# Decode attention over cached pages: pages turned in 32x32 blocks on VectorE, block-diagonal queries, one softmax join, and memory keys as fp32 products

## What is computed

```python
# decode tokens: attention over 1024 cached positions (8 pages of 128) and the token itself
q_lat = einsum("bqhe,rhe->bqhr", q_nope, w_uk)              # 256 wide
s_past = einsum("bqhr,bkr->bhqk", q_lat, c_past) + einsum("bqhe,bke->bhqk", q_pe, kpe_past)
s_new  = einsum("bqhr,bkr->bhqk", q_lat, c_new)  + einsum("bqhe,bke->bhqk", q_pe, kpe_new)
p = softmax(concatenate([s_past, s_new], -1) * MLA_SCALE)
o = einsum("bqhr,rhe->bqhe", p_past @ c_past + p_new @ c_new, w_uv)
# prompt: memory keys and values, 256 tokens, 2048 -> 4 heads x 128
mn = rms_norm(mem, norm_mem); mem_k = mn @ w_mk; mem_v = mn @ w_mv
```

## Time and profile before

| | |
|---|---|
| runs of the kernel before | 1203.07, 1203.53, 1209.15 us; median 1203.53 us |
| the profiled execution | 1201.51 us, of which the span from first to last instruction is 1199.8 us |
| granted TensorE clock, mean | 0.992 of full speed |
| DMA | 216.13 MB, mean 180 GB/s |

### The profile page before, as it was taken

How to read it: one execution, slowest core, us unless ns; L and a number is a source line. 1 busy time by engine, 2 the same in 40 slices (tenths; PEclk the granted TensorE clock), 3 DMA queues, 4 the chain that set the end, 5 groups by cost and what they waited for, 6 DMA issues and landing times. The chain is left out here.

```text
span 1199.8 us, 25822 instructions
## 1 busy us (share of the span) xinstructions
PE 1151.4 (96%) x10209; PEld 1062.3 (89%) x10209; DVE 894.3 (75%) x1521; ACT 643.3 (54%) x1130; POOL 172.8 (14%) x282
## 2 busy tenths in 40 slices
PE   7999999999999999998889999999998999999988
PEld 6999999999777899997879999999986779999977
DVE  5689988889767544686587998888997773448745
ACT  7474454545457544565565645444446664446554
POOL 1210101010353000032011010101014510001400
PEclk9999999999999999999989999999999999999999
DMA  7795756464568466687447676655654874667842
GB/s 209 189 264 141 220 136 179 123 186 134 166 189 241 140 183 177 198 252 264 119 114 202 186 190 171 177 150 153 172 150 142 224 212 140 186 184 219 275 176 73
DMA packets 318971, 216.13 MB, mean 180 GB/s; under 512 B 21620, under 2 KB 300512, under 8 KB 318298
## 3 DMA queue, kind: packets, MB, share of 16 engines
q1 hardware_dynamic: 301728, 164.64, 49.9%
q0 software_dynamic: 16800, 49.83, 13.3%
q10 hardware_dynamic: 330, 0.11, 0.0%
HBM read 209.31 MB, written 7.15 MB: 180 GB/s over the span
## 5 line engine op out<-in xcount | busy, mean ns | idle before, releaser
L1341 ACT ACTIVATE whi<-stage 128x2048 fp32r<-128x2048 f32 (+2 forms) x157 | 272.9, 1739 | 276.6 <-PE U L691 234.5
L1963 DVE TENSOR_TENSOR wlo<-stage,whi 128x2048 fp32r<-128x2048 f32 x138 | 315.8, 2289 | 129.8 <-ACT whi L1341 129.6
L689 PE MATMUL U<-Ahi,whi 128*128 128x264 f32 x1152 | 333.3, 289 | 0.7 <-DVE wlo L1963 0.5
L690 PE MATMUL U<-Alo,whi 128*128 128x264 f32 x1152 | 326.9, 284 | 0.0
L691 PE MATMUL U<-Ahi,wlo 128*128 128x264 f32 x1152 | 326.3, 283 | 0.0
L689 PEld LDWEIGHTS U<-Ahi,whi 128*128 128x128 f32 x1152 | 217.4, 189 | 4.5 <-DVE wlo L1963 1.6
L690 PEld LDWEIGHTS U<-Alo,whi 128*128 128x128 f32 x1152 | 217.7, 189 | 0.0
L691 PEld LDWEIGHTS U<-Ahi,wlo 128*128 128x128 f32 x1152 | 216.4, 188 | 0.0
L2140 DVE SCALAR_TENSOR_TENSOR acc<-uext,cwall,acc 128x256 f32<-128x256 f32 x464 | 189.2, 478 | 0.4
L689 PE MATMUL U<-Bhi,whi 128*128 128x264 f32 x384 | 108.9, 284 | 0.0
L690 PE MATMUL U<-Blo,whi 128*128 128x264 f32 x384 | 108.8, 283 | 0.0
(11 more groups left out here) (461 smaller groups left out, 2176.2 us busy)
## 6 DMA issues: line engine op xcount, KB each, us to landing
stage<-in_w_in SPq DMA_DIRECT2D x76, 1024.0 KB, 6.0
stage<-in_w_out SPq DMA_DIRECT2D x32, 1024.0 KB, 5.8
stage<-in_w_mk SPq DMA_DIRECT2D x8, 1024.0 KB, 6.5
cp<-in_cache_kv_latent POOLq DMA_DIRECT2D x64, 128.0 KB, 3.1
cp<-in_cache_kv_latent SPq DMA_DIRECT2D x64, 128.0 KB, 3.0
stage<-in_w_mv SPq DMA_DIRECT2D x8, 1024.0 KB, 5.4
Kt<-in_cache_mem_k POOLq DMA_DIRECT2D x16, 512.0 KB, 6.4
stage<-in_w_xq SPq DMA_DIRECT2D x8, 1024.0 KB, 7.1
```

The lines of the kernel that those rows point to most:

```text
L689: mm(bk[:, 0:cols], whi[:, s, w], hi[:, k, :], start=(k == 0), stop=False)
L690: mm(bk[:, 0:cols], whi[:, s, w], lo[:, k, :], start=False, stop=False)
L1341: return A_(out, in_, ACT.Copy, scale=scale)
L1963: ins = V.tensor_tensor(wlo[:, s, :], stage[:, s, :], whi[:, s, :].bitcast(F32), ALU.subtract)
```

## The change

Decode attention goes by sequence s (a "sample", eight pages) instead of chunks of four sequences. VectorE turns each page in 32x32 blocks (`key_turns`: 2560 elements on each partition a sample, from `rawc` and `rawk` to `KBL` and `KBP`, of which there is one copy). Queries are spread once (`spread_queries`: 40 products with columns of the identity) and copied by ScalarE into `QB`, which POOL has set to zero, so that each block of 32 rows of a 128x32 weight tile holds its queries in its own 8 columns. `scores(s)` then makes 40 products of 64 columns, and every row of the result (page pair, block, head) has its own maximum and sum. Each sample's values go unscaled to `oR[s]`; at the end `stats_turn`, `combine_max`, `combine_weights`, `weights_turn`, `combine_pick` and `latents` join all rows of all samples with the new token's scores. Copies of probabilities and values move from VectorE to ScalarE (`d_probs`, `d_out`). The 8 loads of `dmask` go.

The memory rows stay in fp32 (`memF`, even ones by ScalarE, odd ones by VectorE: `mem_full`), and a quarter of a memory key unit is four fp32 products that take the weights from `stage`. These units are not split; their stage buffers are free when the unit is done. For the memory value units, `memF` is split later, in the loop over output units (ScalarE for m = 4 to 7, VectorE for m = 5 to 8).

The core of the diff:

```diff
-    CPO = ((W, W + 4096), (W + 10240, W + 14336), (M, M + 8704))
-    KRO = (W + 8192, W + 18432, M + 4096)
-    cp = [[at(f"cp{e}_{pp}", [P, 4, KVL], CPO[e][pp]) for pp in range(PP)] for e in range(3)]
-    kr = [at(f"kr{e}", [P, PP, 4, DR], KRO[e]) for e in range(3)]
-    KT = at("KT", [P, 2, 4, KEYS], W + 30336)
-    KTr = at("KTr", [P, 2, KEYS], W + 38528)
-    sD = at("sD", [P, KEYS + NB], W + 40960)
+    RAW = (W, W + 10240, W + 30720)
+    rawc = [at(f"rawc{e}", [P, NPAGE, KVL], RAW[e]) for e in range(3)]
+    rawk = [at(f"rawk{e}", [P, NPAGE, DR], RAW[e] + 8192) for e in range(3)]
+    KBL = at("KBL", [P, NPAGE, RBL, 32], W + 20480)
+    KBP = at("KBP", [P, NPAGE, RBP, 32], W + 28672)
...
         def load(l, u, s, dst, src):
 
-            sp.wait_ge(split_hi.sem, split_hi.at(l, u - NST + 1))
-            sp.wait_ge(split_lo.sem, split_lo.at(l, u - NST + 1))
+            if U_MK <= u - NST < U_MK + 4:
+                sp.wait_ge(unit_done.sem, unit_done.at(l, u - NST + 1))
+            else:
+                sp.wait_ge(split_hi.sem, split_hi.at(l, splits(u - NST)))
+                sp.wait_ge(split_lo.sem, split_lo.at(l, splits(u - NST)))
...
             load_mk(1)
             if l == 0:
-                sp.wait_ge(const_load, 16 * 12)
+                sp.wait_ge(const_load, 16 * 4)
             load_pages(sp, l, 0, 0)
             load_pages(sp, l, 1, 0)
-            load_mk(2)
             load_pages(sp, l, 2, 0)
             load_pages(sp, l, 3, 0)
-            load_mk(3)
+            load_mk(2)
             load_pages(sp, l, 4, 0)
             load_pages(sp, l, 5, 0)
+            load_mk(3)
+            load_pages(sp, l, 6, 0)
             load_out(0)
-            load_pages(sp, l, 6, 0)
+            load_pages(sp, l, 7, 0)
             load_out(1)
-            load_pages(sp, l, 7, 0)
             load_out(2)
...
+            wait_apart(pool, unit_done.sem, unit_done.at(l, U_MK))
+            nc.gpsimd.memset(QB[:, :, :, :], 0.0)
+            nc.gpsimd.memset(pD[:, :, :, :, :], 0.0).then_inc(qb_zero.sem, 1)
...
+            def spread_queries():
+                pe.wait_ge(ql_ev.sem, ql_ev.at(l, 4))
+                pe.wait_ge(qn_ev.sem, qn_ev.at(l, H))
+                pe.wait_ge(ut_ev.sem, ut_ev.at(l, 2))
+                for k in range(RBK):
+                    for i in range(4):
+                        if k < RBL:
+                            sel, q = ident[:, 32 * (k % 4):32 * (k % 4) + 32], QLt[:, k // 4, :, :]
+                        else:
+                            sel, q = ident[0:DR, 32 * (k - RBL):32 * (k - RBL) + 32], QPt[0:DR, :, :]
+                        last = mm(HAB[32 * i:32 * i + 32, 64 * k:64 * k + 64], sel, q, start=True, stop=True)
+                last.then_inc(qb_mm.sem, 1)
...
+            def scores(s):
+                pe.wait_ge(kb_rdy.sem, kb_rdy.at(l, s + 1))
+                if s % 4 == 0:
+                    pe.wait_ge(qb_ev.sem, qb_ev.at(l, s // 4 + 1))
+                if s >= 2:
+                    pe.wait_ge(dex.sem, dex.at(l, s - 1))
+                o = 64 * (s % 2)
+                for k in range(RBK):
+                    for g in range(4):
+                        keys = KBL[:, 2 * g:2 * g + 2, k, :] if k < RBL else KBP[:, 2 * g:2 * g + 2, k - RBL, :]
+                        last = mm(HC[32 * g:32 * g + 32, o:o + 64], QB[:, s, k, :], keys, start=(k == 0), stop=(k == RBK - 1))
...
+            def probs(s):
+                pe.wait_ge(dex.sem, dex.at(l, s + 1))
+                if s >= 2:
+                    pe.wait_ge(dpT_ev.sem, dpT_ev.at(l, s - 1))
+                for t in range(2):
+                    o = 64 * (s % 2) + 32 * t
+                    for i in range(4):
+                        last = mm(HD[32 * i:32 * i + 32, o:o + 32], sD[:, s % 2, 32 * t:32 * t + 32],
+                                  ident[:, :].rearrange("p (g i h) -> p i g h", g=4, i=4)[:, i, :, :], start=True, stop=True)
...
+            def latents():
+                pe.wait_ge(cm_dve.sem, cm_dve.at(l, CM_PICK))
+                pe.wait_ge(do_ev.sem, do_ev.at(l, NB))
                 for c in range(2):
-                    last = tr(HD[:, c * P:(c + 1) * P], oR[:, c * P:(c + 1) * P], ident[:, :])
-                last.then_inc(doT_mm.sem, 1)
+                    w = slice(c * P, (c + 1) * P)
+                    mm(HB[:, c * 64:c * 64 + 64], cnew[:, w], cnd[:, :, :], start=True, stop=False)
+                    for s in range(NB):
+                        last = mm(HB[:, c * 64 + s * H:c * 64 + (s + 1) * H], oR[s][:, w], csel[:, s, :],
+                                  start=False, stop=(s == NB - 1))
+                last.then_inc(cm_pe.sem, 1)
...
+                bk = U[s % 2]
                 if s == 0:
-                    pe.wait_ge(mn_lo.sem, mn_lo.at(l, 14 if k0 == 0 else 16))
-                part(U_MK + s, s, Ahi[:, :, 0:NM], Alo[:, :, 0:NM], k0, k0 + 4)
+                    pe.wait_ge(mn_act.sem, mn_act.at(l, 4))
+                    pe.wait_ge(mn_dve.sem, mn_dve.at(l, 3 if k0 < 12 else 4))
+                if k0 == 0:
+                    u = U_MK + s
+                    pe.wait_ge(stage_full[s % 2], l * (16 * NU // NST) + u * (16 // NST) + (16 - s % 2 * (16 // NST)))
+                    pe.wait_ge(u_evac.sem, u_evac.at(l, u - 1))
+                for k in range(k0, k0 + 4):
+                    last = mm(bk[:, 0:NM], stage[:, s % 2, k * P:(k + 1) * P], memF[:, k, 0:NM],
+                              start=(k == 0), stop=(k == KC - 1))
+                if k0 == 12:
+                    last.then_inc(unit_done.sem, 1)
...
+            spread_queries()
+            memory_columns(2)
             pe.wait_ge(conv_done.sem, conv_done.at(l, H))
             group([convY[:, c, :] for c in range(4)], True, False)
             group([convY[:, c, :] for c in range(4, CC)], False, True).then_inc(part_mm.sem, 1)
...
-            memory_columns(2)
+            memory_columns(3)
+            new_scores()
+            memory_columns(4)
+            memory_columns(5)
+            combine(4, 3)
+            memory_columns(6)
+            memory_columns(7)
...
+            sample(0, mks(0), mks(1), mks())
+            sample(1, then(lambda: pe.wait_ge(mean_rdy.sem, mean_rdy.at(l, 1)), mks(2)), mks(3),
+                   then(mks(4), lambda: squares_sum(0), lambda: squares_sum(1)))
+            sample(2, mks(5), then(lambda: combine(5, 4), mks(6)), mks(7))
+            sample(3, mks(8), mks(9), mks(10))
+            sample(4, mks(11), mks(12), mks(13))
+            sample(5, mks(14), mks(15), mks())
+            sample(6, lambda: out_part(0, 0, 2), lambda: out_part(0, 2, 4), lambda: out_part(1, 0, 2))
+            scores(NB - 1)
+            out_part(0, 4, 6)
+            probs(NB - 1)
+            stats_turn()
+            out_part(1, 2, 4)
+            values(NB - 1)
+            out_part(0, 6, CC)
+            weights_turn()
+            out_part(1, 4, 6)
+            latents()
...
+            def query_blocks(half):
+                act.wait_ge(qb_mm.sem, qb_mm.at(l, 1))
+                act.wait_ge(qb_zero.sem, qb_zero.at(l, 1))
+                b = slice(4 * half, 4 * half + 4)
+                for i in range(4):
+                    r = slice(32 * i, 32 * i + 32)
+                    ins = copy(QB[r, b, :, NB * i:NB * i + NB],
+                               HAB[r, 0:64 * RBK].rearrange("p (k b h) -> p b k h", k=RBK, b=NB)[:, b, :, :])
+                ins.then_inc(qb_ev.sem, 1)
...
+            d_probs(5)
             ln_scale(6)
             ln_upper(3)
+            hi(U_MK + 4, 0)
+            d_out(5)
             d_exp(6)
...
+            ln_scale(7)
             ln_upper(4)
+            d_probs(6)
             mk_unit(3)
...
-            ln_scale(7)
             ln_upper(5)
+            d_out(6)
+            hi(U_MK + 5, 1)
+            d_exp(7)
+            d_probs(7)
             ln_upper(6)
-            d_exp(7)
...
+            act.wait_ge(cm_dve.sem, cm_dve.at(l, CM_DIFF))
+            A_(cexp[:, :], cexp[:, :], ACT.Exp, scale=SCALE).then_inc(cm_exp.sem, 1)
             ln_upper(7)
+            d_out(7)
...
+                if 4 <= m < 8:
+                    q = slice(4 * m - 16, 4 * m - 12)
+                    act.wait_ge(mfd_lo.sem, mfd_lo.at(l, 2))
+                    copy(Alo[:, q, 0:NM], memF[:, q, 0:NM]).then_inc(mem_hi.sem, 1)
...
+            def key_turns(s):
+                if s == 0:
+                    dve.wait_ge(st_conv, l * 32 + 32)
+                for hf in range(2):
+                    dve.wait_ge(cp_load[hf][s % 3], 128 * (l * (3, 3, 2)[s % 3] + s // 3 + 1))
+                    if s and hf == 0:
+                        dve.wait_ge(ds_mm.sem, ds_mm.at(l, s))
+                    g = slice(4 * hf, 4 * hf + 4)
+                    V.transpose(KBL[:, g, :, :].rearrange("p g k a -> p (g k a)"), rawc[s % 3][:, g, :].rearrange("p g r -> p (g r)"))
```

(38 more changed lines are left out.)

595 lines of the change are left out of this document (218 added, 377 removed).

## The result

The changed kernel takes 1222.05 us (median of four, 1216.40 to 1226.14) beside 1204.04 us for the kernel before: a ratio of 1.0144, 95% interval 1.0108 to 1.0179. Measured once more with later runs it is 1.0125 (1.0103 to 1.0147). So it is slower by 15 to 18 us, and the range of 1187 to 1210 us did not hold it.

A forecast was written before the change was run, and what follows sets the result against it. TensorE's own queue bounds the kernel: 11.2 us less work a layer against waits grown by 9 to 12 us, taken as 1.0 us faster a layer, so 1201.5 us against the median 1203.5; 8-in-10 range 1187 to 1210 us.

The forecast's parts named there:

- the fp32 quarter: Memory keys on TensorE: four fp32 products take 1.78 us against 1.51, 0.28 us more, 16 times, 4.5 us a layer.
- The latents: End of the decode stage on TensorE: 18 fp32 products at 0.22 us, 4.0 us a layer.
- ahead of unit 1: TensorE waits 4.75 us a layer for the split of the second w_out unit, its high half queued behind `d_out(6)`.
- ahead of unit 0: TensorE comes 2.6 us early a layer, waiting for the split of the first w_out unit.
- ahead of memory columns 4: TensorE waits 0.75 us a layer for ScalarE's `mem_full(2)`, behind `query_blocks(0)` and POOL's memset of QB.
- the wait for the stores of uT: `key_turns(0)` on VectorE waits until they land, taken as 322 us; TensorE then waits 1.8 us for `mem_full(3)`.
- `values(6)`: Sample 6 on TensorE: `probs(6)` and this wait 1.4 us more, as `d_max(6)` is queued behind the first w_out unit's low half.
- the tail: End of the decode stage: dependent VectorE and ScalarE steps for maxima, weights and pick make 3.3 us of waits a layer.
- The waits don't come: Rival: waits at the decode stage's start and tail stay away, 3 to 7 us a layer more gained, 1191.5 us; chance 0.26.
- All gained: Rival: all removed TensorE work is gained, 22.4 us, giving 1181 us; chance 0.05.
- Late pages: Rival: page loads come late, four or five samples wait about 1.5 us each, 1214.5 us (1208 at half); chance 0.22.
- The hold of 2.37 us: In the kernel before, POOL's load at 346.51 stood 2.37 us with no releaser while VectorE ran a low-half split.

The follow-up runs named there:

- the reordered one: Changed kernel with scores, probabilities and statistics turn of sample 7 put ahead of the second w_out unit, VectorE's maximum of sample 7 earlier: ratio 0.9973, 1199.4 us.
- the stalled kernel before: Kernel before, with TensorE held ahead of the second w_out unit in each layer by 45 chained GpSimd fills: ratio 1.0156, 1221.8 us.
- the runs with unread products: fp32 products nobody reads put in TensorE's waits: changed kernel, longest wait 1.0139, all longer waits 1.0117; the reordered one, remaining waits 1.0017.

## Why the prediction was wrong, point by point

**Work.** The changed kernel's TensorE work at full clock can be read from the reordered one: 74.1 us of busy time at a mean clock of 0.98, so 72.5 to 74.1 us, against 82.4 before. I forecast 11.2 us less per layer; it is 8.3 to 9.9. The term that was short is the fp32 quarter, 1.93 us and not 1.78, 2.4 us a layer: its price was right where it stood alone in the kernel before (0.27 us), and I took a row whose neighbours were other than those of the new order. The latents were short by some 0.5 us (4.6 us at full clock for 4.0). The scores came as said (359.96 to 361.21, 1.25 us). The 0.5 us a quarter that I had counted from the four passes of true fp32 in the Trainium skill ("FP8 and Floating Point Precision", TensorE Precision Notes) were not borne out by the run with fp32 keys alone.

**Waits.** Forecast 15.3 us a layer, measured 11.1 and 12.2 of idle time. The dearest came as worked out: 4.62 for 4.75 ahead of unit 1, 2.60 for 2.6 ahead of unit 0, 0.86 for 0.75 ahead of memory columns 4. Too high: the wait for the stores of uT, which landed in 2.4 us and not in 5.6, so it is nothing in layer 0 and 1.37 us in layer 1 for 1.8; `values(6)` 0.66 for 1.4; the tail 2.5 (1.17, 0.70, 0.38, 0.29) for 3.3. So I had the work 1.3 to 2.9 us too good and the idle time less grown than my sum: +7.4 and +8.5, where I said 9 to 12. Together that is 2.5 us less to 0.2 more a layer, with the forecast of 1.0 less in it.

**The step that failed** is one that I left out: that behind the new waits every instruction costs what its row at 1.00 says. The kernel before has no fall in this stage, and I wrote the 4.75 us down as 4.75 us. A row that prices one does stand in its trace, between the two layers, and the forecast did not use it: behind 9.41 us of idle time the clock is at 0.50, and 6 us of work run at half speed.

```profile
604.42 0.56 PE L705 MATMUL U<-Ahi,whi 128*128 128x264 f32 x1 [9.41 <-DVE Alo L2530]
```

```profile
604.40:610.40 6.00, 5.97 (x29) 4.84 (x30) 5.93 (x8) 5.58 (x8) 0.00 (x0) 0.50 0.00 0
```

Busy time shows the size: 79.5 and 83.3 us, for work of 72.5 to 74.1, are 5 to 11 us a layer of running at half clock, and 2 to 4 us more behind each stage. The price is a term for each wait, the wait itself plus the work that follows at half speed; the stalled kernel before shows it in a clean place, 9.4 us for a stall of 6.84. The second fall, at the latents, hangs on no single wait, and its cause stays open.

**Rivals.** "The waits don't come" is out: the order set the large ones, as said against it. All gained is out too. Late pages, the rival that I gave for a slower kernel, came close to the time by another way: TensorE waits on no page in samples 1 to 5 (VectorE's turns do once in layer 0, for 0.52 us at 346.44). The Trainium skill's rule on GpSimd and VectorE locking each other out ("SBUF — State Buffer", Who interferes with whom) decides nothing here: beside the block transposes GpSimd's loads took 0.54 us each, as in the kernel before. The hold of 2.37 us on which I had built this rival stands in the changed kernel too, ahead of the load at 342.76, while VectorE is idle, so VectorE's work did not cause it there. What the chances lacked was a slower case from TensorE itself.

**The marks.** Page turns gone, 10 to 15 us idle in the stage with the largest ahead of unit 1 by `wlo`, 2 to 3 us ahead of unit 0, scores at 1.3: right. About 11 us less work: 8.3 to 9.9. Fp32 quarters at 1.8: wrong. VectorE idle until the stores of uT land: wrong in layer 0, right in layer 1 (1.89 us). Of the signs of a wrong forecast that I named, none is the one that came.

**Still open.** What sets off a fall is not settled (see below). Cross-attention of layer 0 takes 17.4 us before, in the reordered kernel and in the second trace of the changed kernel, but 18.8 in its first and 21.4 and 23.2 in two of the runs with unread products; memory pages that land late and the clock both show in it. A change of 5 us in the decode stage shifts when they are asked for, and I didn't separate the two. The spread among the executions of the changed kernel (10 us) is likely of the same kind, which was not shown.

## What to carry to other kernels

A wait on TensorE, where it bounds the kernel, has two prices: its length, and the work behind it at half clock, which these traces show behind every wait of 4.6 us or more in this stage and behind some of 1.2 to 3 us; look at the granted clock of the windows behind each long wait, and move independent work into it before trimming short ones. Work that fills a wait must be work that is to be done anyway: unread products kept the clock up and gave little back. Small products in different column groups should go round the groups, not group by group.
